# Query, key and value projections of the second attention: weight blocks at rest, three token pieces moving

## What is computed

```python
def _stick_breaking(h, pos, w_in, w_out, k_past, v_past):
    q, k, v, g = jnp.split(h @ w_in, 4, axis=-1)        # h = rmsnorm(x)
    ...
    z = jnp.einsum('bqhd,bkhd->bhqk', qb, kf) * (B_DH ** -0.5)
    valid = k_pos[None, :] < qpb[:, None]
    log_keep = jnp.where(valid, jax.nn.log_sigmoid(-z), 0.0)
    after = lax.cumsum(log_keep, axis=3, reverse=True) - log_keep
    a = jnp.where(valid, jnp.exp(jax.nn.log_sigmoid(z) + after), 0.0)
    o = jnp.einsum('bhqk,bkhd->bqhd', a, vf)
    o = o * jax.nn.silu(g)
    return o @ w_out, k, v
```

## Time and profile before

| what | value |
|---|---|
| median of three runs | 2007.91 us (2007.61 to 2008.26) |
| the profiled execution | 2002.79 us |
| its span, first to last instruction | 2000.9 us |
| mean granted TensorE clock | 0.982 |
| the second attention | about 955 to 1765 us of the span |
| one steady group | 95.0 us |

### The profile page before, as it was taken

One profiled execution on the slowest core, in us unless ns is written; L12 is line 12 of the kernel. 1 busy time (PEld: TensorE's weight loads), 2 busy tenths in 40 slices (PEclk: granted clock), 3 DMA queues, 4 the chain that ended last, 5 costly groups with the idle time before them and its releaser, 6 DMA issues. The chain is left out here.

```text
span 2000.9 us, 31736 instructions
## 1 busy us (share of the span) xinstructions
PE 1874.5 (94%) x11429; PEld 1618.4 (81%) x11429; DVE 1122.8 (56%) x2269; ACT 1060.5 (53%) x2556; POOL 387.5 (19%) x597
## 2 busy tenths in 40 slices
PE   4999999999999899997699999999999999899996
PEld 4887878878788689997588887878788888689995
DVE  5456455564564632356156667675757575843545
ACT  5455454564554532354166666675767575732345
POOL 0132231331313100255001011111111111100341
PEclk8999999999999899999799999999999999999999
DMA  4121112211211233121110212111111011242113
GB/s 155 51 71 38 49 49 60 64 39 48 67 53 53 97 98 103 51 84 54 53 39 23 65 35 63 38 49 38 54 33 60 27 60 49 77 134 89 53 53 127
DMA packets 161803, 125.07 MB, mean 63 GB/s; under 512 B 10992, under 2 KB 152624, under 8 KB 161648
## 3 DMA queue, kind: packets, MB, share of 16 engines
q1 hardware_dynamic: 160784, 122.85, 20.1%
q10 hardware_dynamic: 864, 0.20, 0.0%
HBM read 89.49 MB, written 33.52 MB: 61 GB/s over the span
## 5 line engine op out<-in xcount | busy, mean ns | idle before, releaser
L107 PE MATMUL pj<-area,h_high 128*128 128x384 f32 (+1 forms) x2304 | 649.5, 347 | 26.4 <-issue 11.3
L107 PEld LDWEIGHTS pj<-area,h_high 128*128 128x128 f32 (+1 forms) x2304 | 407.2, 181 | 50.4 <-issue 11.5
L107 PE MATMUL pj<-area,h_low 128*128 128x384 f32 (+1 forms) x1152 | 390.5, 339 | 0.0
L107 PEld LDWEIGHTS pj<-area,h_low 128*128 128x128 f32 (+1 forms) x1152 | 210.0, 182 | 8.9
L1530 POOL TENSOR_TENSOR lb_o<-lb_o,lb_keep 128x512 f32<-128x512 f32 (+3 forms) x80 | 77.7, 971 | 588.1 <-ACT lb_keep L1230 585.2
L1375 DVE SCALAR_TENSOR_TENSOR lb_s<-lb_sc,lb_m 128x512 f32<-128x512 f32 (+4 forms) x200 | 109.8, 549 | 75.1 <-ACT lb_m L1211 75.1
L1201 ACT ACTIVATE lb_m<-lb_sc 128x512 f32<-128x512 f32 (+4 forms) x200 | 87.5, 487 | 70.8 <-PE lb_sc L1612 41.7
L455 ACT ACTIVATE la_p<-la_sc,la_nm 128x128 f32<-128x128 f32 (+5 forms) x144 | 105.7, 737 | 33.8 <-DVE la_nm L652 32.9
L1408 DVE TENSOR_TENSOR lb_s_low<-lb_s,lb_s_high 128x512 fp32r<-128x512 f32 (+1 forms) x192 | 119.8, 624 | 6.6
L1186 ACT ACTIVATE lb_tok<-pj,norm_token 128x128 f32<-128x128 f32 (+1 forms) x72 | 26.4, 367 | 178.5 <-PE pj L107 178.5
L1406 DVE CAST lb_s_high<-lb_s 128x512 fp32r<-128x512 f32 (+1 forms) x192 | 103.7, 540 | 25.7 <-DVE lb_s L1375 0.5
(11 more groups left out here) (307 smaller groups left out, 4504.3 us busy)
## 6 DMA issues: line engine op xcount, KB each, us to landing
stage<-in_a_w_in SPq DMA_DIRECT2D x60, 192.0 KB, 3.6
stage<-in_b_w_in SPq DMA_DIRECT2D x60, 192.0 KB, 3.1
stage<-in_ple_w_gate SPq DMA_DIRECT2D x22, 512.0 KB, 3.8
h_low<-o_t SPq DMA_DIRECT2D x14, 528.0 KB, 6.6
mix_b_xs<-x_mid SPq DMA_DIRECT2D x8, 528.0 KB
lift_xt<-in_x SPq DMA_DIRECT2D x8, 512.0 KB, 4.2
stage<-in_a_w_in SPq DMA_DIRECT2D x16, 256.0 KB, 5.1
out_ak<-la_tok SPq DMA_DIRECT2D x8, 512.0 KB, 3.3
```

The costliest lines, as they stand in the source:

```text
L107: last = pe.matmul(out, x, y, start=start and n == 0, stop=stop and n == 2, **kw)
```

## The change

The projection is turned round and cut into nine **slots** `x`: three token pieces (384, 384 and 288 columns of `h`) by three kinds (`x % 3`: query, key, value). In a slot the 128x128 weight block of one kind rests and the tokens of one piece move. The result has features on partitions. VectorE multiplies it out of PSUM into a new buffer `tmp` by the norm's row (`slot_norm`). For queries and keys ScalarE takes the high part from `tmp` (`slot_high`) and VectorE the low part (`slot_low`). For keys and values TensorE turns the slot back with three transposes (`turn`) and ScalarE copies them into `tok` (`tokens`), which no longer holds queries. The bank of a query slot is free after `slot_norm`, that of a key or value slot after `tokens`. Slots 0 to 5 stand where tiles 0 to 5 stood, slots 6 to 8 where tiles 6 to 8 stood.

```diff
+            def slot_norm(at, x):
+                dve.wait_ge(S["pj_tok"], at.nth("pj_tok", x + 1))
...
+                row = norm["row"][:, cols_of(x)]
+                if kind(x) == 0:
+                    ins = dve.scalar_tensor_tensor(out=slot_tmp(x), in0=slot_bank(x), scalar=DH ** -0.5, in1=row,
+                                                   op0=ALU.mult, op1=ALU.mult)
+                else:
+                    ins = dve.tensor_tensor(slot_tmp(x), slot_bank(x), row, ALU.mult)
+                ins.then_inc(S["slot_normed"], 1)
@@ VectorE, visit i
-                    if i < 4:
-                        turned_low(at, 5 + i)
+                    if 1 <= i <= 2:
+                        slot_low(at, i + 5)
+                    if i <= 2:
+                        slot_norm(at, i + 6)
...
-                    if more and 8 <= i <= 12:
-                        turned_low(ahead, i - 8)
+                    if more and i in (8, 9, 11, 12):
+                        slot_low(ahead, i - 8)
+                    if more and i in (7, 8, 9, 10, 11, 13):
+                        slot_norm(ahead, min(i - 7, 5))
@@ VectorE, prologue
-            for t in range(AHEAD - 1):
-                turned_low(Count(table, 0), t)
+            for x in range(AHEAD):
+                slot_norm(Count(table, 0), x)
+                if x > 0 and kind(x - 1) < 2:
+                    slot_low(Count(table, 0), x - 1)
@@ TensorE
-                    last = three(pe, pj[0:n, t % 2, 0:NQ], [x[:, k, rows] for x in h], [x[:, k, :] for x in w],
+                    last = three(pe, slot_bank(x), [y[:, k, f] for y in w], [y[:, k, cols_of(x)] for y in h],
...
+            def slot_free(at, x):
+                if kind(x) == 0:
+                    pe.wait_ge(S["slot_normed"], at.nth("slot_normed", x + 1))
+                else:
+                    pe.wait_ge(S["tok_ready"], at.nth("tok_ready", kv_nth(x)))
...
+            def turn(at, x):
+                pe.wait_ge(S["slot_normed"], at.nth("slot_normed", x + 1))
+                for n in range(3):
+                    m = TILES[3 * (x // 3) + n][1]
+                    last = pe.transpose(pj[0:m, x % 2, n * P:(n + 1) * P], tmp[:, x % 3, n * P:n * P + m], ident[:, :])
@@ TensorE, visit i: the turns move behind the sums
-                    if i < 4:
-                        turn(at, i + 5)
-                    if more and 8 <= i <= 12:
-                        turn(ahead, i - 8)
...
+                    if i in (0, 2, 3):
+                        turn(at, i + 5)
+                    if more and i in (9, 10, 12):
+                        turn(ahead, i - 8)
@@ ScalarE, visit i
                     if i == 0:
-                        turned_high(at, 5)
                         act.wait_ge(S["pv"], at.before("pv"))
-                        tokens(at, 6)
+                        tokens(at, 5)
...
                     if i == 2:
-                        turned_high(at, 7)
+                        slot_high(at, 7)
+                        tokens(at, 7)
+                    if i == 3:
                         tokens(at, 8)
```

More of the change, by code:

```diff
@@ L1056, in stick_layer @@
         gate_bank = lambda c: pj[:, (c + 1) % 2, 0:GC]
-        turned_bank = lambda t: pj[:, t % 2, 0:2 * P].rearrange("p (a n) -> p a n", a=2)[:, :, 0:TILES[t][1]]
-        tile_cols = lambda t: slice(t * P, t * P + TILES[t][1])
+        kind = lambda x: x % 3
+        cols_of = lambda x: slice(PIECES[x // 3][0], PIECES[x // 3][0] + PIECES[x // 3][1])
+        slot_bank = lambda x: pj[:, x % 2, 0:PIECES[x // 3][1]]
+        slot_tmp = lambda x: tmp[:, x % 3, 0:PIECES[x // 3][1]]
+        qk_nth = lambda x: 2 * (x // 3) + kind(x) + 1
+        kv_nth = lambda x: 2 * (x // 3) + kind(x)
         chunk = lambda c: slice(CHUNKS[c][0], CHUNKS[c][0] + CHUNKS[c][1])
-        by_token = lambda t, part: norm["token"][0:TILES[t][1], part, t:t + 1]
         def bank(s):
@@ L1294, in body @@
                     if i == 2:
[L1295 removed]
+                        slot_high(at, 7)
+                        tokens(at, 7)
+                    if i == 3:
                         tokens(at, 8)
[L1297 to L1298 removed]
                     if more:
[L1300 to L1305, removed]
+                        if i == 8:
+                            slot_high(ahead, 0)
+                        if i == 9:
+                            slot_high(ahead, 1)
+                            next_tokens(1)
+                        if i == 10:
+                            next_tokens(2)
+                        if i == 11:
+                            slot_high(ahead, 3)
                         if i == 12:
[L1307 to L1309 removed]
+                            slot_high(ahead, 4)
+                            next_tokens(4)
                 if not more:
@@ L1318, in _ @@
                 split_gate(0, half_)
[L1319 to L1322, removed]
+            for x in range(AHEAD - 1):
+                if kind(x) < 2:
+                    slot_high(Count(table, 0), x)
+                if kind(x) > 0:
+                    tokens(Count(table, 0), x)
             act.wait_ge(S["fill"], 1 + 1)
@@ L1353, in split_gate, with slot_low @@
                 dve.tensor_tensor(wg[1][:, ks, :], raw_gate, wg[0][:, ks, :].bitcast(F32), ALU.subtract).then_inc(S["gw_low"], 1)
[L1355 to L1359, removed]
+            def slot_norm(at, x):
+                dve.wait_ge(S["pj_tok"], at.nth("pj_tok", x + 1))
+                if kind(x) < 2:
+                    dve.wait_ge(S["qk_low"], at.nth("qk_low", qk_nth(x - 3)) if x >= 3 else at.before("qk_low"))
+                if kind(x) > 0:
+                    dve.wait_ge(S["turned"], at.nth("turned", kv_nth(x - 3)) if x >= 3 else at.before("turned"))
+                row = norm["row"][:, cols_of(x)]
[5 more added lines that the diff above has]
+                ins.then_inc(S["slot_normed"], 1)
+            def slot_low(at, x):
+                dve.wait_ge(S["qk_high"], at.nth("qk_high", qk_nth(x)))
+                dve.tensor_tensor(qk[1][:, kind(x), cols_of(x)], slot_tmp(x), qk[0][:, kind(x), cols_of(x)].bitcast(F32),
+                                  ALU.subtract).then_inc(S["qk_low"], 1)
             def body(r, more):
@@ L1658, in values @@
                     pe.wait_ge(S["a"], at.nth("a", through(i)))
+                    pe.wait_ge(S["tok_ready"], at.all("tok_ready") if c == 2 else at.nth("tok_ready", 2 * (b // 3) + 2))
                     if i == 0:
@@ L1696, in gate_project, with free_bank @@
                         last.then_inc(S["g_ready"], 1)
[L1698 to L1702, removed]
-                    else:
-                        pe.wait_ge(S["g_normed"], at.nth("g_normed", t + 2))
+                def free_bank(x):
+                    if x < 2:
+                        pe.wait_ge(S["g_normed"], at.nth("g_normed", x + 2))
+                    else:
+                        which = at if x >= AHEAD else ahead
+                        slot_free(which, x - 2)
                 for i in range(NP + 1):
@@ L1761, in _ @@
             first = Count(table, 0)
[L1762 to L1769, removed]
+            for x in range(AHEAD):
+                if x >= 2:
+                    slot_free(first, x - 2)
+                project(first, x, 0)
+                if x > 0 and kind(x - 1) > 0:
+                    turn(first, x - 1)
+                project(first, x, 1)
+                if x == 0:
                     pe.wait_ge(S["gw_low"], first.all("gw_low"))
```

58 lines of the change are left out of this document (30 added, 28 removed).

## The result

The changed kernel takes 1990.09 us (median of 4 runs, 1988.53 to 1991.66), the kernel before 2007.76 us beside it (4 runs, 2004.3 to 2008.26). The ratio is 0.9913, with a 95% interval of 0.9902 to 0.9925: 17.7 us less, between 15 and 20. The forecast was 22.5 us less, to 1985.4 us. Range and direction held; the gain came out a fifth short.

What follows compares the result with a forecast made beforehand. TensorE, busy for 94% of the span, was taken as the bound, with round trips between engines deciding in the prologue. 16.0 us from the groups plus 6.5 from the prologue made 22.5 off 2007.9: 1985.4 us, range 1976.5 to 1994.

Steps and rivals of the forecast that it cites:

- Step 1: TensorE's projection blocks: three blocks of 288 columns instead of 384 in slots 6 to 8 save 3.04 us per group.
- weight loads set the spacing: Rival: 288-column matmuls come every 176 ns like those of 384, only the prologue gains, 2001.4 us; chance 0.04.
- Step 2: TensorE's transposes per group: seven pairs before against five triples after, 1.3 against 1.4 us, so nothing.
- Step 3: Visit 0: TensorE waits 1.1 us longer at pair 0's suffix sums, so slot 6's saving of 1.04 us is worth nothing.
- everything arrives: Rival: visit 0 takes nothing back, 3.04 us in each of eight groups plus 6.5, 1977.1 us; chance 0.10.
- Step 4: Visits 1 to 3: slots 7 and 8 keep their 2.0 us in all eight groups, 16.0 us.
- signs of being wrong: Waits at transposes, more waits for the soft plus's low part in visits 8 to 12, or 288-column blocks of 4.2 us.
- Step 5: VectorE 4.3 us busier per group, ScalarE relieved: neither the bound, cost 0, at most 3 us; visit 8's cover 0.2 us.
- Step 6: Prologue: round-trip waits of 7.4 us go, a new 1.0 us wait comes before the first scores; gain 6.5 us.

Runs made afterwards that it cites:

- all_384: The changed kernel with the third piece also moving 384 columns, 96 of them for nothing, turns and norms unchanged: 2001.70 us.
- turn_place: The changed kernel with its transposes put back between the values product and the suffix sums: 1989.62 us.
- fill_wait: The changed kernel with half of slot 7's block issued ahead of the suffix sums of pair 0 instead of behind them: 1972.19 us.
- after_again: The changed kernel run once more without alteration, as base of its batch: 1992.70 us.
- fill_and_order: fill_wait plus, in the prologue, VectorE making the previous slot's low part ahead of the next slot's norm: 1971.57 us.
- norm_twice: The changed kernel with every slot's norm made a second time on VectorE into a buffer nothing reads: 1991.30 us.

## Why the prediction was right, and where it fell short

**Step 1 held.** Blocks of 288 columns take 3.20 us where 3.19 was taken from the last phase (3.27 and 3.28 right behind a turn), and all_384 gives the 2.0 us back per group. The rival that weight loads set the spacing falls with it. By the sustained rule of the Trainium skill (TensorE: Matmul & The Clock Gate, "Back-to-back issue gap") a block would have lost 0.3 us, the estimate of step 1; here the trace disagrees with that rule, with 1.0 us.

**Step 2 failed**, by its word "nothing". The triples cost what was said, 0.24 to 0.30 us. But they were priced by themselves, and not by what they do to the work behind them: a turn that stands between the column sums and a block makes that block 0.1 us longer (4.29 against 4.20 us in turn_place). The trace of before had the sign of it, a block of 4.28 us behind its turn, but the forecast took its blocks from elsewhere. So slots 7 and 8 bring 1.5 us per group and not 2.0, 8 x 0.5 = 4 us in all, the largest part of what was missed; all_384 shows the same 0.5 us with the columns put back. By experiment 0.2 of the 0.5 is the turns' place: putting them where they were brings that much. Five triples behind the values product cost 5 x 0.30 = 1.5 us against 1.4 for the seven pairs before, and what is left then, some 0.2 us, is spread over many steps in hundredths of a us. For those no cause was tried.

**Step 3 held.** The block behind the suffix sums of pair 0 starts 8.58 us into the group, before 8.59. The wait came out at 0.27 + 1.18 us, for the 1.5 forecast. fill_wait shows the other half of the statement: slot 6's saving was there and was taken by the wait. The rival "everything arrives" is what that kernel reaches in the length of a group: 94.98 - 91.86 = 3.1 us less, where the rival had 3.04.

**Step 4** was right in kind: visits 1 to 3 keep slots 7 and 8. The last group doesn't: from 1673.38 to 1764.77 it took 91.39 us before, from 1659.41 to 1750.55 it takes 91.14 after. The lower clock level holds in it for 10.6 us after (6.8 from 1705.8 on, and from 1746.7 to the end) and for 3.9 before, but that isn't enough to explain it: after_again's last group has 3.5 us at that level and takes 91.0 us as well. What both have, and before doesn't, are two waits late in the group, in visits 11 and 12 (TensorE's timeline after):

```profile
1733.42 0.41 PE L1672 MATMUL lb_sc<-lb_s_high,lb_tri 128*128 128x384 f32 x1 [0.88 <-DVE lb_s_low L1429]
...
1738.31 0.36 PE L1672 MATMUL lb_sc<-lb_s_high,lb_tri 128*128 128x256 f32 x1 [0.60 <-DVE lb_s_low L1429]
```

They make 1.5 us (after_again's other late waits are those of before, within 0.1 us each), and they are one of the signs of being wrong that the prediction named, in this one group of eight. turn_place's last group lacks them and takes 89.0 us. fill_wait has them (91.0 us) and fill_and_order hasn't (88.2 us), though their lists in this group are the same; so why they come stays open.

**Step 5 held**, by norm_twice. The new operations cost what the nearest rows said, 7.8 us per group for nine norms and six low parts. VectorE as a whole is busy 28.7 us longer and not the 35 forecast: a group grew by 3.6 us (61.93 to 65.56) where 4.3 were forecast, for which no cause was sought. VectorE's timeline in visit 8, at the place where the cover was thin:

```profile
1438.14 0.55 DVE L1379 TENSOR_TENSOR lb_qk_low<-lb_tmp,lb_qk_high 128x384 fp32r<-128x384 f32 x1
1438.61 0.55 DVE L1374 TENSOR_TENSOR lb_tmp<-pj,norm_row 128x384 f32<-128x384 f32 x1
1439.30 0.69 DVE L1446 TENSOR_TENSOR lb_o<-lb_acc,lb_o 128x512 f32<-128x512 f32 x1
```

The norm ends at 1439.16 and the add follows at 1439.30; the values product it adds ended 1439.18 (the next matmul begins there). The hole of 0.90 us is filled and the cover just reached.

**Step 6 held** for the waits. From the prologue's second block to the first scores it was 1006.73 - 975.37 = 31.4 us and is 1002.43 - 977.35 = 25.1, with one stretch of 3.4 us at the lower clock level in each: 6.3 us for the 6.5 forecast, and the new wait is 1.03 us for 1.0. VectorE's timeline shows its cause as the step put it, a norm ahead of the low part:

```profile
1001.26 0.56 DVE L1374 TENSOR_TENSOR lb_tmp<-pj,norm_row 128x384 f32<-128x384 f32 x1 [3.52 <-PE pj L107]
1001.74 0.55 DVE L1379 TENSOR_TENSOR lb_qk_low<-lb_tmp,lb_qk_high 128x384 fp32r<-128x384 f32 x1
```

TensorE's timeline at the first and the second block of the prologue, before and after:

```profile
960.25 0.66 PE L107 MATMUL pj<-area,h_high 128*128 128x384 f32 x1 [5.83 <-issue]
...
975.37 0.45 PE L107 MATMUL pj<-area,h_high 128*128 128x384 f32 x1 [2.56 <-DVE lb_wg_low L1353]
```

```profile
962.59 0.98 PE L107 MATMUL pj<-h_high,area 128*128 128x384 f32 x2 [5.83 <-issue]
...
977.35 0.62 PE L107 MATMUL pj<-h_high,area 128*128 128x384 f32 x2 [2.12 <-DVE lb_wg_low L1361]
```

The last clause of step 6, "nothing comes from the clock", was argued for the prologue and let stand for the whole kernel. In the groups the clock did count: two stretches of 1.5 us in place of one in this pair, a number that differs between executions.

**The sum.** The profiled pair lies 14.3 us apart, 8.2 short of the forecast. Of those, 2.0 us were lost ahead of all this: the prologue's second block starts at 977.35 and not at 975.37, since its first one does so 2.3 us later, behind work that the change leaves alone. In the profiles of the other changed kernels that first block starts anywhere from 961.5 to 965.9 us, so this is no cost of the change. In this pair the eight groups are 8.8 us shorter (758.3 to 749.5); with the new wait of 1.03 us, which lies in group 0 and is step 6's, put aside, their term is 9.8 us instead of 16.0. Of the missing 6.2, about 4 are step 2's, 1.5 the second stretch at the lower level, and the last group kept 1.3 less than the others. The seventh group of before, which was 0.4 longer than its neighbours, gives some of it back. The medians, at 17.7, lie 4.8 short: the profiled execution of before lay 5.0 us under its median, that of after 1.6.

## What to carry to other kernels

Price a saved column or matmul only up to the next wait that already stands on that engine: what is saved ahead of it is lost until other work is put into the gap, and then the gap comes in whole (1.6 us per group here, the half block that was moved forward). When a small step is moved, price it together with what stands behind it in its new place. Compare two profiles by stretches at the same granted clock, and count the others apart.

## What the runs showed that was not expected

- A projection block right behind plain transposes is 0.1 us longer (4.29 and 3.28 against 4.20 and 3.20 us; 4.28 in the kernel before), while the transposes are shorter behind column sums (0.24) than behind the values product (0.30).
- TensorE's clock fell to the lower level for 3.4 us at a time with TensorE busy for 98% and more of the group around it (93.12 of 95.00 us, 94.64 of 95.06), at two places of a group alone: right behind a wait of 1.2 us, and some 3 us behind the start of 30 matmuls that move 32 columns. With the idle time at the first of them taken away all four stretches stood at the second, where after_again had two at each (one execution of either). Each costs 1.5 to 1.6 us, and their number differs between executions.
